# Loading expert weights sooner while the mixer still runs, and split pieces by rows: one layer of a hybrid S5 / differential-attention / mixture-of-experts block

## The reference, cut to what matters

```
xn = rms_norm(x, norm1_g);  z = xn @ w_in            # 1024 x 4096: u, q, k, v, g_ssm, g_att
y_ssm = s5_branch(u)                                  # state space, in chunks; then * sigmoid(y @ w_glu + b)
y_att = diff_attention(q, k, v)                       # 4 heads, two softmaxes each, chunk-causal
mixed = sigmoid(g_ssm) * (y_ssm @ w_proj_ssm) + sigmoid(g_att) * (y_att @ w_proj_att)
h = x + mixed @ w_out
hn = rms_norm(h, norm2_g);  logits = hn @ w_router + b_router      # 32 experts, top 4, softmax weights
per expert e, for its tokens:
  hup = hn @ w_up[e] + b_up[e]                        # 1024 x 2048, 8 MiB
  act = clipped SwiGLU of the even and odd columns
  out += weight * (act @ w_down[e] + b_down[e])       # 1024 x 1024, 4 MiB
y = h + out
```

## Time and profile before

| | us |
|---|---|
| median of 3 runs | 1144.63 |
| lowest, highest | 1144.61, 1145.05 |
| profiled execution | 1145.06 |
| its span on the core | 1143.3 |
| PE busy, share | 1097.3, 96% |
| DMA: bytes, mean rate | 435.13 MB, 381 GB/s |

### The profile page before, as it was taken

How to read it: one execution, slowest core, us unless ns; L and a number is a source line. 1 busy time by engine, 2 the same in 40 slices (tenths; PEclk the granted TensorE clock), 3 DMA queues, 4 the chain that set the end, 5 groups by cost and what they waited for, 6 DMA issues and landing times.

```text
span 1143.3 us, 14281 instructions
## 1 busy us (share of the span) xinstructions
PE 1097.3 (96%) x5292; PEld 447.7 (39%) x5292; DVE 294.3 (26%) x802; ACT 175.0 (15%) x347; POOL 34.1 (3%) x51
## 2 busy tenths in 40 slices
PE   7999999999999999999999999999999999999997
PEld 4468887633333333333333333333333333333332
DVE  5986244242111111111111111111111111111111
ACT  3432440221111111111111111111111111111110
POOL 5120010000000000000000000000000000000000
PEclk9999999999999999999999999999999999999999
DMA  7744489999999999999999999999999999999996
GB/s 217 192 142 102 122 270 356 369 372 390 429 426 428 428 429 428 427 429 428 429 428 429 428 427 429 428 429 428 429 429 428 428 428 429 428 430 428 428 428 269
DMA packets 63578, 435.13 MB, mean 381 GB/s; under 512 B 19856, under 2 KB 28096, under 8 KB 38592
## 3 DMA queue, kind: packets, MB, share of 16 engines
q1 hardware_dynamic: 57776, 433.17, 92.7%
q0 software_dynamic: 608, 1.34, 0.5%
q10 hardware_dynamic: 5168, 0.27, 0.3%
HBM read 432.01 MB, written 1.57 MB: 379 GB/s over the span
## 4 chain that ended last, share of the span: by engine, by line
PE 58%; DMA 38%; DVE 2%; issue 1%; ACT 0%; SPq 0%; DVEq 0%; ACTq 0%
DMA arena<-in_w_up 38%; PE bank L1067 23%; PE bank L1112 9%; PE bank L636 5%; PE bank L674 4%; PE bank L620 3%; PE bank L1011 2%; PE bank L996 2%; PE bank L950 2%; PE bank L874 1%; PE bank L859 1%; PE bank L847 1%; DMA arena<-in_w_in 1%; PE bank L806 1%; PE bank L938 1%
## 5 line engine op out<-in xcount | busy, mean ns | idle before, releaser
L1067 PE MATMUL bank<-arena 128*64 128x512 f32 x2048 | 452.6, 594 | 30.2 <-DMA arena<-in_w_up 29.9
L1067 PEld LDWEIGHTS bank<-arena 128*64 128x64 f32 x2048 | 143.7, 137 | 331.8 <-issue 271.8
L1112 PE MATMUL bank<-arena 128*64 128x512 f32 x1024 | 226.8, 595 | 0.0
L1817 DVE TENSOR_SCALAR arena<-bank 128x256 f32<-128x256 f32 x64 | 27.2, 425 | 499.9 <-PE bank L1067 499.9
L1112 PEld LDWEIGHTS bank<-arena 128*64 128x64 f32 x1024 | 70.7, 137 | 133.9 <-issue 133.1
L1383 ACT ACTIVATE arena<-arena 128x256 f32<-128x256 f32 x64 | 26.6, 417 | 451.7 <-DVE arena L1818 451.7
L620 PEld LDWEIGHTS bank<-arena 128*128 128x128 f32 (+1 forms) x450 | 49.3, 143 | 88.6 <-issue 80.9
L620 PE MATMUL bank<-arena 128*128 128x128 f32 (+1 forms) x450 | 75.3, 290 | 8.1 <-DMA arena<-in_x 5.0
L1011 PE MATMUL bank<-arena 64*128 64x512 f32 x256 | 63.9, 616 | 0.7 <-ACT arena L1391 0.7
L996 PE MATMUL bank<-arena 128*64 128x512 f32 x248 | 60.1, 605 | 0.0
L1391 ACT ACTIVATE arena<-bank 128x512 f32<-128x512 f32 x32 | 19.1, 597 | 256.6 <-PE bank L1112 256.6
(11 more groups left out here) (295 smaller groups left out, 521.3 us busy)
## 6 DMA issues: line engine op xcount, KB each, us to landing
arena<-in_w_up SPq DMA_DIRECT2D x125, 2048.0 KB, 25.5
arena<-in_w_down SPq DMA_DIRECT2D x63, 2048.0 KB, 26.8
arena<-in_w_in SPq DMA_DIRECT2D x16, 1024.0 KB, 5.7
arena<-in_w_up SPq DMA_DIRECT2D x5, 1024.0 KB, 6.0
arena<-in_w_out SPq DMA_DIRECT2D x4, 1024.0 KB, 7.8
arena<-in_w_proj_ssm SPq DMA_DIRECT2D x8, 256.0 KB, 6.0
arena<-in_w_proj_att SPq DMA_DIRECT2D x2, 1024.0 KB, 8.2
arena<-in_w_down SPq DMA_DIRECT2D x2, 1024.0 KB, 31.0
```

The source lines that it names most:

```text
L1067: last = pe.matmul(B[n][64 * h:64 * h + 64, :], xg[:, 2 * j + r, :], rows[r][2 * h + n], start=False, stop=(j == order[-1] and r == 1), sk ...
L1112: last = pe.matmul(B[3][64 * n:64 * n + 64, :], (actT_last if last_block else actT)[:, k % 4, k // 4, :], dn_w[parity][k // 4][:, k % 4, 5 ...
L1817: TS(part(glu_t, n), v[:, 0], LIMIT, None, ALU.min)
```

## The change

Six edits, all in what SP issues and when, and one in which wait of PE covers what.

- Pieces 16 to 18 are still four DMAs of 256 KiB, but one per q instead of one per t: each fills one quarter of all 128 partitions.
- Up tile 0 of block 0 is issued ahead of piece 16, behind a wait for `y_ps` 2. Up tiles 1, 2, 3 follow pieces 17, 18, 19.
- The waits behind piece 16 go; the one for `yT_ps` 2 stands ahead of block 0's down tiles.
- Up tile 2 of block 1 is loaded in two halves by row: row 0 when `mixed` is 4, row 1 where the whole tile was loaded. Row 0 counts into `ahead_in`, which block 1 now awaits (96) at its first tile instead of its second.
- The four loads of `b_up` go ahead of the wait for `out_ps` 3.
- Tile 2 of block 3 is issued when block 1 has used its tile 2 (`up_used` 5), ahead of the row and tile 1 of block 2, and tile 3 of block 3 stays where both were (`up_used` 8).

```diff
@@ piece(i) @@
             if i == 16:
-                return [(v[32 * t:32 * t + 32], w[P * t:P * t + P].rearrange("(q r) n -> r q n", q=4))
-                        for t in range(4)]
+                return [(v[:, q, :],
+                         w.rearrange("(t q r) n -> q t r n", t=4, q=4)[q]) for q in range(4)]
...
@@ SP @@
-            ups_after = {17: (0,), 18: (1,), 19: (2,), 23: (3,)}
+            ups_after = {17: (1,), 18: (2,), 19: (3,)}
...
+                if i == 16:
+                    sp.wait_ge(s["y_ps"], 2)
+                    load_up_tile(0, 0, 0, 0)
                 if i == PIECES - 1:
...
-                if i == 16:
-
-                    sp.wait_ge(s["y_ps"], 1)
-                    sp.wait_ge(s["yT_ps"], 2)
...
+                if i == 23:
+                    sp.wait_ge(s["yT_ps"], 2)
                 for j in downs_after.get(i, ()):
                     load_dn(0, 0, 0, j)
-            def load_row(dst, e, r):
-
-                return sp.dma_start(dst, w_up[e, 0:2 * P, :].rearrange("(p r) (h n) -> r p h n", r=2, h=2)[r])
+            def load_row(dst, e, r, j=0):
+
+                return sp.dma_start(dst, w_up[e, 2 * P * j:2 * P * (j + 1), :]
+                                    .rearrange("(p r) (h n) -> r p h n", r=2, h=2)[r])
...
             sp.wait_ge(s["mixed"], 4)
+            load_row(up_w[1][SHARED][:, 0], 1, 0, SHARED).then_inc(s["ahead_in"], 16)
             load_ahead_part(3)
             load_dn(1, 1, 1, 0)
-            sp.wait_ge(s["out_ps"], 3)
             for q in range(4):
                 sp.dma_start(bup[E * q:E * q + E], b_up[:, 512 * q:512 * q + 512]).then_inc(bup_in, 16)
+            sp.wait_ge(s["out_ps"], 3)
             load_dn(1, 1, 1, 1)
             sp.wait_ge(s["out_ps"], 5)
-            load_up_tile(1, 1, 1, SHARED)
+            load_row(up_w[1][SHARED][:, 1], 1, 1, SHARED).then_inc(up_in[1][SHARED], 16)
             load_ahead_part(2)
...
             load_downs(2, 2, 0)
+            sp.wait_ge(s["up_used"], UT + ORDER.index(SHARED) + 1)
+            load_up_tile(3, 3, 1, SHARED)
             sp.wait_ge(s["up_used"], UT + ORDER.index(0) + 1)
             load_row(up_w[0][0][:, 0], 2, 0).then_inc(up_in[0][0], 16)
             sp.wait_ge(s["up_used"], UT + ORDER.index(1) + 1)
             load_up_tile(2, 2, 0, 1)
-            load_ahead(3, 3, 1)
+            sp.wait_ge(s["up_used"], 2 * UT)
+            load_up_tile(3, 3, 1, SHARED + 1)
             load_downs(3, 3, 1)
@@ PE, expert_block @@
                     elif j < SHARED:
-                        if ahead and j == 0:
-                            pe.wait_ge(s["ahead_in"], 80)
-                        else:
+                        if not (ahead and j == 0):
                             pe.wait_ge(up_in[parity][j], 16 * b + 16)
                     else:
 
+                        if ahead and j == SHARED:
+                            pe.wait_ge(s["ahead_in"], 16 * 6)
                         pe.wait_ge(up_in[parity][j], 8 * b + (8 if parity else 16))
```

## The result

The changed kernel is slower: 1162.81 us (median of 5, 1161.86 to 1163.45) against 1145.0 us, ratio 1.0157 with a 95% interval of 1.0145 to 1.0169. The prediction was 1143.1 with 1141.8 to 1144.9 as its range, so it missed in sign and in size. The profiled execution took 1161.86 us, 16.8 us more than the one before, with a span of 1160.1.

The account below looks back on a forecast made before the run. PE paces blocks 1 to 8, the transfer stream later blocks, so the stream must start earlier. Edits 1 to 5 0.0, edit 6 -2.6, next gate +1.0, restart +0.1: -1.5, median 1143.1 us, range 1141.8 to 1144.9.

Parts of the forecast that it names:

- Edit 4: Split pieces, each of four loads filling all 128 partitions instead of 32: taken as zero, with 6.9 us of margin.
- The bound I set: Split pieces in the new form: at worst four loads one after another, 13 to 26 us a piece.
- The place where it bites: Slowness of the split pieces would count once the second projection piece lands after 173.0, 18.0 us after its first issue.
- Rival C: Split pieces: one piece's loads run one behind the other, PE waits 8.0 us, 1151.1 us in all; chance 0.06.
- the gain of 1.5: Whole kernel: all terms together make it 1.5 us faster, shifting the stream, the stalls and the tail.
- Edits 1, 2, 3, 5: Sooner up tiles, moved y waits, odd tile in two rows with sooner bias loads: 0.0 us.
- The margin of the GLU piece: GLU piece behind the first up tile: lands by about 145, read by ACT at 150.36, 5 us of margin.
- Edit 6: Block 3's tile issued 10.5 us sooner, filling the dry place at 268 to 276: -2.6 us, +1.0 given back, +0.1 restart.
- at 295.07, 9.6, slack 1.9: Load issued at 295.07 lands 9.6 us later; against 7.7 into an idle queue, 1.9 us of slack.
- the least slack decides: Gates behind the filled dry place: the smallest slack, 1.6 us at 284.77, limits the gain that passes.
- Rival B: Block 3's tile: hidden anyway or not in time, 0 to 0.9 us pass, 1144.2 us as middle; chance 0.18.
- The weighed rule: 2 MiB load estimated at 6.8 us unqueued, slack 2.5 at 284.77, 1142.1 us; the prediction held to 7.7.

Follow-up runs that it names:

- e9_second_piece_new_only: The changed kernel with the new load form on the second projection piece only, the GLU and first projection pieces in the old form: 1153.15 us, ratio 1.0080.
- e4_block3_tile_only: The kernel before with only block 3's tile 2 issued sooner, at its own space's first use: 1144.97 us, ratio 1.0006.
- e1_old_pieces: The changed kernel with the split pieces loaded as before, four loads by 32 partitions each: 1144.4 us, ratio 1.0000.
- e5_early_edits_only: The kernel before with sooner up tiles and bias loads and the odd tile in two rows; old pieces, block 3's tile unmoved: 1145.22 us, ratio 1.0008.
- the first experiments: Follow-up runs of altered kernels, timed beside the kernel before; the text does not list which ones count as first.

## Why the prediction was wrong

**Edit 4 was taken at zero and cost 16 to 18 us, and it is the whole result.** That is the step that failed. I wrote that the split pieces "keep their bytes and their runs of 2 KiB" and took zero, from the `in_w_proj_att` row as the nearest. Bytes and runs were indeed the same as in that row, and so were the 128 partitions; the number of engines was not, four instead of sixteen. That row's source has 128 outer rows beside 128 partitions, the new form has 4 beside 128. What I should have compared is the outermost dimension on both sides. The bound I set, 13 to 26 us a piece, holds the 13.8 us of the GLU piece, and the second piece took 32.1 (153.03 to 185.14). That is luck: it was put together from four starts, and what is paid is bytes on four engines, 10.3 us a piece, and queue. The place where it bites was right.

**Rival C, at 0.06, was the outcome**: a PE wait at the second half of `w_proj_ssm`, block 0 and the whole stream later with it, 1151.1 forecast and 1162.8 measured. Its mechanism was wrong: had the loads gone one after the other, each with its own start, the share would fall between them, and it stands at 0.26 throughout. My reason against it, that nothing in the diff puts a wait between them, did not touch the mechanism that worked. It came out 12 us short. PE waited 13.3 us and not 8.0, because I priced the second piece alone, while the GLU and the first projection piece stand ahead of it in the same form (in the new form alone, in `e9_second_piece_new_only`, the second piece held PE's products up by 0.35 us); the idle PE then ran at the lower clock for 2.3 us, other waits added 2.0, the stream ran 1.0 longer, and the gain of 1.5 that I had taken off did not come.

**Edits 1, 2, 3, 5 at nothing**: right, 830.15 against 830.33 for the stream's part and a ratio of 1.0008 (0.9999 to 1.0017). The margin of the GLU piece was right in the old form only.

**Edit 6, -2.6 and +1.0 given back**: the first number is right, the hole of 268 to 276 closes. The second is not: 2.0 to 2.4 us are given back. At the gate of 284.8, from which I took my least slack, the landing came down from 9.3 to 7.7 in `e4_block3_tile_only`, so the figure and the 1.6 us held there (it was 9.0 in `e1_old_pieces` and 8.0 in the changed kernel). The step that failed is "at 295.07, 9.6, slack 1.9", which puts the same 7.7 under the next gate. With a hole ahead of it the load there lands in 8.8, 9.3 and 9.4 in the three, so its slack was 0.2 to 0.8 us, and "the least slack decides". (Up to 0.3 of that is scatter: 9.3 in `e5_early_edits_only`, with no hole there.) Rival B had just this reading, with the uneven spacing of the landings as its reason, a slack of near 1 and 1144.2 as its middle; without edit 4 it would have been the outcome. Why a landing behind a hole varies between 7.7 and 9.4 us is open.

**The weighed rule** (a fixed part of roughly 2 us, from the Trainium skill's page "SBUF — State Buffer", section "The DMA setup-cost knee") pointed the wrong way: 2 MiB behind a hole landed in 7.7 to 9.4 us, where the estimate by it was 6.8. The rule that spoke against this change was the one cited above, of the page "DMA: Bandwidth & Descriptors".

## What to carry to other kernels

When a load's access pattern is rewritten, compare the outermost dimension of source and destination, not only bytes, run length and partitions; in the profile a constant DMA share of 2, 4 or 8 sixteenths gives the number of engines away at once, where nothing but such loads is under way. A load on few engines also delays those behind it, so its own landing is not its whole price. And a hole filled in a transfer stream is a gain only up to the slack of the next gates; take that slack from landings at those gates, and expect the tail to have one too.

## What the runs showed that I had not expected

The first eight products of 512 columns take 5.43 us in the profiled execution before and 3.67 in the changed kernel's, with all of the mixer then 2.0 us earlier (18.45 instead of 20.43). Of the changed kernel's five runs the profiled one is the fastest by 0.85 us, which makes the profiles differ by 16.8 and the medians by 17.8 us. The same products before, then in the changed kernel:

```profile
9.88 5.43 PE L636 MATMUL bank<-arena 128*128 128x512 f32 x8 [0.95 <-DMA arena<-in_w_in]
```

```profile
9.65 3.67 PE L642 MATMUL bank<-arena 128*128 128x512 f32 x8 [1.06 <-DMA arena<-in_w_in]
...
18.45 48.23 PE L642 MATMUL bank<-arena 128*128 128x512 f32 x112
```

The kernel before itself, over 27 runs beside the first experiments, spread from 1143.11 to 1147.27 us, far more than the three runs shown at first (0.44 us). Effects of under 1 us had to be read in the profiles, by differences of two events, and the 1.0 us by which the changed kernel's stream ran longer than before's is of the size of that scatter. It is lost in one place, at about 340 to 346 us: the down tile issued at 327.7 still lands in 12.2 us (12.3 for the same load before), the next one in 14.9 (14.0). Why is open.
